# Up products of a convolutional FFN: seven-product pairs in groups of two, and one written order for the end of the stage

## The reference

```python
def conv_ffn(x, w_up, conv_w, conv_b, w_down):      # x 512 x 1024
    h = x @ w_up                                     # 1024 -> 5632
    h = depthwise_causal_conv(h, conv_w) + conv_b    # three taps along the sequence
    gate, val = jnp.split(h, 2, axis=-1)
    return (jax.nn.silu(gate) * val) @ w_down        # 2816 -> 1024
```

## Time and profile before

| | |
|---|---|
| median of 3 runs | 2039.16 us (2037.84 to 2039.9) |
| the profiled execution | 2042.29 us, of which the span from first to last instruction is 2040.6 us |
| PE busy | 2026.4 us, 99% of the span |
| DVE busy | 1619.3 us, 79% |
| ACT busy | 1115.0 us, 55% |
| POOL busy | 433.7 us, 21% |
| granted TensorE clock | full in all 40 slices |

### The profile page before, as it was taken

One profiled execution on the slowest core, in us unless ns is written; L12 is line 12 of the kernel. 1 busy time (PEld: TensorE's weight loads), 2 busy tenths in 40 slices (PEclk: granted clock), 3 DMA queues, 4 the chain that ended last, 5 costly groups with the idle time before them and its releaser, 6 DMA issues.

```text
span 2040.6 us, 33333 instructions
## 1 busy us (share of the span) xinstructions
PE 2026.4 (99%) x12636; PEld 1750.7 (86%) x12636; DVE 1619.3 (79%) x2555; ACT 1115.0 (55%) x1861; POOL 433.7 (21%) x482
## 2 busy tenths in 40 slices
PE   9999999999999999999999999999999999999998
PEld 8889998888988899888877888998888889999887
DVE  6668878889467887899888669777997668877898
ACT  4755545447335555546656646555465755545555
POOL 0520332210000232120035402322110520332220
PEclk9999999999999999999999999999999999999999
DMA  8123344384432334467421123334674122334393
GB/s 291 64 104 125 109 130 150 121 255 172 145 129 75 97 105 129 145 190 243 166 73 42 63 83 104 119 104 155 197 237 163 65 104 83 109 122 147 115 269 122
DMA packets 82570, 276.42 MB, mean 135 GB/s; under 512 B 9408, under 2 KB 13632, under 8 KB 82032
## 3 DMA queue, kind: packets, MB, share of 16 engines
q1 hardware_dynamic: 59184, 214.67, 30.4%
q0 software_dynamic: 11200, 24.12, 5.8%
q10 hardware_dynamic: 12032, 35.54, 4.8%
HBM read 256.43 MB, written 14.73 MB: 133 GB/s over the span
## 4 chain that ended last, share of the span: by engine, by line
PE 91%; DVE 5%; DMA 2%; ACT 1%; issue 0%; DVEq 0%; ACTq 0%; SPq 0%
PE ps L2437 12%; PE ps L2438 12%; PE ps L2439 12%; PE ps L2649 6%; PE ps L3018 5%; PE ps L3019 5%; PE ps L3020 5%; PE ps L2976 5%; PE ps L2978 5%; PE ps L2977 5%; PE ps L2509 2%; PE ps L2465 2%; PE ps L2466 2%; PE ps L2467 2%; DMA raw<-slabs 2%; PE ps L2497 1%
## 5 line engine op out<-in xcount | busy, mean ns | idle before, releaser
L2437 PE MATMUL ps<-h_hi,w_hi 128*128 128x512 f32 (+1 forms) x1104 | 433.0, 392 | 0.0
L2438 PE MATMUL ps<-h_lo,w_hi 128*128 128x512 f32 (+1 forms) x1104 | 429.6, 389 | 0.0
L2439 PE MATMUL ps<-h_hi,w_lo 128*128 128x512 f32 (+1 forms) x1104 | 428.9, 389 | 0.0
L1603 DVE TENSOR_TENSOR w_lo<-raw,w_hi 128x1024 fp32r<-128x1024 f32 x300 | 372.0, 1247 | 39.1 <-ACT w_hi L901 35.5
L901 ACT ACTIVATE w_hi<-raw 128x1024 fp32r<-128x1024 f32 x312 | 326.4, 1053 | 133.1 <-DVE raw L2251 74.0
L2437 PEld LDWEIGHTS ps<-h_hi,w_hi 128*128 128x128 f32 x1104 | 207.6, 188 | 44.0 <-issue 4.0
L2439 PEld LDWEIGHTS ps<-h_hi,w_lo 128*128 128x128 f32 x1104 | 207.3, 188 | 43.2
L2438 PEld LDWEIGHTS ps<-h_lo,w_hi 128*128 128x128 f32 x1104 | 207.7, 188 | 38.9
L1281 ACT ACTIVATE work<-ps,conv_sb 128x512 f32<-128x512 f32 x120 | 93.0, 775 | 162.6 <-PE ps L2439 133.2
L3018 PE MATMUL ps<-w_hi,h_hi 128*128 128x512 f32 x408 | 159.7, 391 | 2.1 <-DVE w_lo L1603 2.1
L3020 PE MATMUL ps<-w_hi,h_lo 128*128 128x512 f32 x408 | 158.8, 389 | 0.0
(11 more groups left out here) (365 smaller groups left out, 5054.6 us busy)
## 6 DMA issues: line engine op xcount, KB each, us to landing
raw<-slabs SPq DMA_DIRECT2D x368, 512.0 KB, 4.1
act<-slabs POOLq DMA_DIRECT2D x64, 256.0 KB, 5.6
bias<-slabs SPq DMA_DIRECT2D x16, 512.0 KB, 6.3
x_dram<-x ACTq DMA_DIRECT2D x16, 512.0 KB, 5.0
x<-x_dram ACTq DMA_DIRECT2D x16, 512.0 KB, 4.9
raw<-act POOLq DMA_DIRECT2D x28, 256.0 KB, 3.3
act<-slabs SPq DMA_DIRECT2D x12, 512.0 KB, 5.4
bias_dram<-bias_rows ACTq DMA_DIRECT2D x2, 2048.0 KB, 12.3
```

The source lines that it names most:

```text
L1603: ve.tensor_tensor(w_lo[:, c % RING, :], raw[:, raw_slot(c), :], w_hi[:, c % RING, :].bitcast(f32), ALU.subtract).then_inc(lo_made, 1)
L2437: pe.matmul(ps[:, bank, cols], hi, h_hi[:, k, cols], start=k == 0, stop=False)
L2438: pe.matmul(ps[:, bank, cols], hi, h_lo[:, k, cols], start=False, stop=False)
L2439: last = pe.matmul(ps[:, bank, cols], lo, h_hi[:, k, cols], start=False, stop=k == KT - 1)
```

## The change

The pairs computed with seven products become 4, 6, 7, 9, 10, 12, 13, 15 and 16: nine per layer in place of seven. Pairs 5, 8, 11, 14 and 17 between them are ordinary. A group is two seven-product pairs f and f+1 and the ordinary pair f+2, and PE interleaves them:

```diff
-FASTS = (FAST_END - FAST) // 2
+FAST_RUNS = 6, 9, 12, 15
+IN_GROUP = 2
+FAST_PAIRS = [FAST] + [q + e for q in FAST_RUNS for e in range(IN_GROUP)]
...
+                p1(FAST)
+                p2(FAST)
+                p6_p5(FAST)
+                p7(FAST)
+                bank_free(FAST + 1)
+                forward(up_slab(L, FAST + 1), 0, up_bank(FAST + 1, 0))
+                p4(FAST)
+                p3(FAST)
+                forward(up_slab(L, FAST + 1, 1), 0, up_bank(FAST + 1, 1))
+                for f in FAST_RUNS:
+                    p1(f)
+                    p2(f)
+                    p6_p5(f)
+                    p7(f)
+                    p1(f + 1)
+                    p2(f + 1)
+                    p4(f)
+                    p3(f)
+                    p6_p5(f + 1)
+                    p7(f + 1)
+                    bank_free(f + 2)
+                    forward(up_slab(L, f + 2), 0, up_bank(f + 2, 0))
+                    p4(f + 1)
+                    p3(f + 1)
+                    forward(up_slab(L, f + 2, 1), 0, up_bank(f + 2, 1))
```

```diff
+                def first_period(f):          # ACT
+
+                    split_hi(up_slab(L, f + 1))
+                    part_hi(f, "x3")
+                    slab_silu(f - 1)
+                    slab_tap(f - 1, 1)
+                    split_hi(up_slab(L, f + 1, 1))
+                    copy(f, 0)
+                    copy(f, 1)
...
+                def period(f):                # DVE, a part
...
+                    part_lo(f + 3, "x1")
+                    part_lo(f + 3, "x3")
+                    slab_gate(f)
+                    part_lo(f + 4, "a11")
+                    slab_tap(f + 1, 1, 1)
+                    c11(f + 3)
+                    x3(f + 4)
+                    slab_tap(f + 1, 1, 0)
+                    c22(f + 3)
...
+                def last_period(f):           # ACT, its end
...
+                    slab_tap(f + 6, 0)
+                    split_hi(DOWN[L] + 2)
+                    operand(L, 3)
+                    slab_silu(f + 6)
+                    slab_tap(f + 6, 1)
+                    split_hi(DOWN[L] + 3)
```

More of the change, by code:

```diff
@@ L709, in _, with load @@
                 ring_slabs(n1 + EARLY, up_slab(L, FAST))
[L710 to L727, removed]
+                def load(q, e):
+                    c = up_slab(L, q, e)
+                    if q - 2 not in FAST_PAIRS:
+                        sp.wait_ge(lo_made, made(c - RAW))
+                    elif e:
+                        sp.wait_ge(part_lo_made["x3"], part_count(L, q - 2, "x3"))
+                        sp.wait_ge(part_lo_made["x4"], part_count(L, q - 2, "x4"))
+                    else:
+                        sp.wait_ge(part_lo_made["x1"], part_count(L, q - 2, "x1"))
+                        sp.wait_ge(up_x2, fast(L, q - 2) + 1)
+                        sp.wait_ge(up_x3, fast(L, q - 2) + 1)
+                    sp.dma_start(raw[:, raw_slot(c), :], slabs[dram(c)]).then_inc(raw_in[raw_slot(c)], 16)
@@ L875, in _ @@
                     at_probs(BASE[L])
-                fourth_sum(L, FAST)
-                for j in range(STEPS - 1):
+                down_sums(L, 0)
+                fourth_sum(L, 4)
+                down_sums(L, 1)
+                fourth_sum(L, 6)
+                fourth_sum(L, 7)
+                down_sums(L, 2)
+                fourth_sum(L, 9)
+                fourth_sum(L, 10)
+                down_sums(L, 3)
+                fourth_sum(L, 12)
+                down_sums(L, 4)
+                fourth_sum(L, 13)
+                down_sums(L, 5)
+                fourth_sum(L, 15)
+                fourth_sum(L, 16)
+                down_sums(L, 6)
+                for j in range(7, STEPS - 1):
                     down_sums(L, j)
-                    if FAST <= 2 * j + 4 < FAST_END and j:
-                        fourth_sum(L, 2 * j + 4)
                 first_sums(L)
@@ new lines, in period @@
+                def period(f):
+                    split_lo(up_slab(L, f + 2))
+                    slab_tap(f - 1, 0, 0)
+                    slab_tap(f, 0, 1)
+                    c11(f + 1)
+                    slab_tap(f - 1, 1, 0)
+                    part_lo(f + 1, "x4")
+                    c22(f + 1)
+                    x1(f + 3)
+                    x1(f + 4)
+                    split_lo(up_slab(L, f + 2, 1))
+                    slab_gate(f - 1)
+                    slab_tap(f, 0, 0)
+                    x2(f + 3)
+                    slab_tap(f, 1, 1)
+                    slab_tap(f + 1, 0, 1)
+                    part_lo(f + 3, "a11")
+                    slab_tap(f, 1, 0)
+                    c12(f + 1)
+                    slab_tap(f + 1, 0, 0)
+                    part_lo(f + 3, "x2")
+                    x3(f + 3)
+                    part_lo(f + 4, "x1")
+                    x2(f + 4)
+                    part_lo(f + 3, "x1")
+                    part_lo(f + 3, "x3")
+                    slab_gate(f)
+                    part_lo(f + 4, "a11")
+                    slab_tap(f + 1, 1, 1)
+                    c11(f + 3)
+                    x3(f + 4)
+                    slab_tap(f + 1, 1, 0)
+                    c22(f + 3)
+                    part_lo(f + 3, "x4")
+                    slab_gate(f + 1)
+                    part_lo(f + 4, "x2")
+                    slab_tap(f + 2, 0, 1)
+                    slab_tap(f + 2, 1, 1)
+                    c12(f + 3)
+                    part_lo(f + 4, "x3")
@@ L2143, in gate, with slab_gate @@
+                def slab_gate(q):
+                    gate(q % 2, q // 2)
                 def gate(c, i):
```

491 lines of the change are left out of this document (318 added, 173 removed).

## The result

| | before | after |
|---|---|---|
| median of the runs | 2039.2 us (2037.84 to 2039.9) | 2053.9 us (2053.21 to 2054.5, 4 runs) |
| ratio, 95% interval | | 1.0073 (1.0055 to 1.009) |
| profiled execution, its span | 2042.3, 2040.6 | 2054.5, 2052.3 |
| mean granted clock | 1.000 | 0.996 |
| matmuls of PE | 12636 | 12924 |

The forecast was 2047.3, with a range from 2042.0 to 2053.5. The direction is right. The time is 6.6 us above the forecast and 0.4 us outside the range, on the side of the first rival, whose figure was 2053.3.

What follows compares the result with a forecast made beforehand. PE, busy 99% of the span, was taken to bound the kernel. Terms of -6.5, +12.1, 0 and +2.5 summed to +8.1 us on the 2039.2 median: 2047.3 us, range 2042 to 2053.5.

Steps and rivals of the forecast that it cites:

- rival 1: PE before p6 of pair 4: the new waits also drop the clock, 6 us more, 2053.3; chance 0.07.
- Term 1: Up stage on PE: two more pairs per layer become cheap, fewer matmuls, 6.5 us saved.
- Term 2: Steady groups of pairs in the up stage: DVE's added work fits with 0.8 us slack, no PE wait, 0.
- Rival 2: Groups in the up stage do not hold, 0.4 us lost in each of 16: +6.4, 2053.7; chance 0.09.
- Term 3: Start of pair 4: ACT's first copy queues behind a waiting SiLU, PE waits 3.0 us per layer, +12.1.
- Rival 3: Start of pair 4: the first copy is not late and p6 starts on time, 2035.2; chance 0.11.
- Term 4: End of up stage: last gate 0.9 us later delays the down product by 0.9, 0.9, 0.7, 0 per layer, +2.5.
- Rival 4: End of the stage helps instead: two present PE waits in the down product vanish, +3.5, 2042.7; chance 0.09.
- The carried difference: Whole kernel: the median taken 3.1 us below the profiled execution, as before the change, so 2050.4 became 2047.3.

Runs made afterwards that it cites:

- e1: The changed kernel with ACT's row at the start of pair 4 put back, first copy ahead of the SiLU: 2040.8 us, ratio 0.9999.
- e4: The changed kernel with the first copy behind SiLU and value tap, ahead of the split: 2049.58 us, ratio 1.0047.
- e7: e1 with the last value tap and last split ahead of operand(L, 3) and the last SiLU at the stage's end: 2034.09 us, ratio 0.9962.
- e11: e7 run once more, on one chip with e9 and e10: 2034.2 us, ratio 0.9968.
- e3: The changed kernel with the first copy right behind the SiLU, ahead of value tap and split: 2044.85 us, ratio 1.0015.
- e6: The changed kernel with 4 more matmuls of 256 columns, result unused, after p2 of pair 4: 2054.34 us, ratio 1.0058.
- e2: The changed kernel with 24 more matmuls of 256 columns, result unused, after p2 of pair 4: 2051.9 us, ratio 1.0057.
- e10: The changed kernel with only the end of the stage changed as in e7, the late first copy left: 2050.84 us, ratio 1.0048.
- e5: The kernel before, with only ACT's row at pair 4 in the changed kernel's order (late first copy): 2056.19 us, ratio 1.0068.
- e8: e7 with POOL's fourth_sum ahead of down_sums again: 2034.5 us, ratio 0.9961.
- e9: e1 run once more, on one chip with e10 and e11: 2040.01 us, ratio 0.9995.

## Why the prediction was wrong in size, by its steps

**Term 1, -6.5: right.** Where no fall comes between (e1 to e4, e7), the stage from p6 to the down product is 1.4 to 1.7 us shorter in each layer (forecast 1.6), and e7 and e11, where nothing else is late, are 8.2 and 6.9 us faster than before by their medians. That holds the 6.5 and a little of the gate that comes earlier.

**Term 2, 0: right.** The period of a group is 31.08 us, the window of a whole group has PE busy throughout, and PE waits nowhere inside the groups. Rival 2 is out. One reading behind this term was wrong, though: full-width low parts do not all stay at 1.22 us beside POOL. In before one takes 1.75 us beside the last of POOL's five instructions for the down product's sums, and beside the same one a half-width part in a group of after takes 1.10 instead of 0.68:

```profile
383.89 1.75 DVE L1603 TENSOR_TENSOR w_lo<-raw,w_hi 128x1024 fp32r<-128x1024 f32 x1
```

```profile
273.96 1.10 DVE L2191 TENSOR_TENSOR a_lo<-raw,a_hi 128x512 fp32r<-128x512 f32 x1
```

That is 0.4 to 0.5 us a time, inside a slack of 0.8; no wait of PE came of it.

**Term 3, +12.1: right in mechanism, place and length.** 2.9 us for 3.0, four times, released by the copy. e3, e4 and e1 take its items away one by one. Rival 3 is out. The rows read 11.6 for the waits themselves, and the distance between the matmuls on both sides gives 12.2.

**The step that failed: pricing these waits at their length.** The prediction kept the clock at its full level because this trace had no wait of that length, put the rival in which the clock drops at 0.07, and sized the sum without it. But a trace with no such wait says nothing for either side. In after the clock falls behind all four waits, 1.4 to 1.5 us each; rival 1 is what happened. That its figure of 1.5 came out is luck: it let the fall last as long as the wait, but after 1.97 us (e4) and 2.44 us (e6) a fall costs the same 1.3 to 1.5. e2 shows the cause (no idle time at p6, no fall there, with all else the same). e3 to e6 and e10 show that falls come with idle times of 2 us and more and not with 1.3, and that from 2 us on the same wait has one or not. "TensorE: Matmul & The Clock Gate" in the Trainium skill, on the clock gate, says that an idle PE falls back to half its clock. The runs agree with the level (0.50 in a window of e5), and the page should have had the larger chance here.

**Term 4, +2.5: the sum right, its layers wrong.** The gate is 0.99 later in every layer (forecast 0.93). The down products of after are longer by 0.47, 0.08, 1.06 and 0.23 us, 1.8 in all, where the forecast had 0.9, 0.9, 0.7 and 0. Over the seven traces with this gate the mean is 2.0, and layer 3, which was to lose nothing, loses most (1.3 on average). So the size came out partly by luck. What failed is the rule that on DVE everything queues behind the gate, with slack that was read in one execution. The split of the earlier trace rows in layer 3 starts 45.98 us after the down product in before, 47.19 in after, and 47.74 in e5, whose gate is where before's is. There DVE had been idle 3 us before that split, waiting for a load of weights:

```profile
1988.58 0.69 DVE L2251 TENSOR_TENSOR raw<-raw 128x512 f32<-128x512 f32 x1 [1.59 <-DMA raw<-slabs]
```

In the other layers the split moves by -0.8 to +1.1 between before and after. A load that lands late takes up the gate's delay or adds its own, so this slack isn't dependable. By the timed pairs the end's order is worth 5 to 6 us for 1.5 us per layer; in proportion 0.99 would cost 3.5 us, an estimate with an interval that holds 2.5. Rival 4 is out: the order helps only with the tap ahead of the operand.

**The carried difference.** The profiled execution of before was 3.1 us above its median, that of after 0.6. Against its own execution the sum gives 2050.4, and 2054.5 was seen: 4.1 short, where the clock alone is 6: the part ahead of the first pair 4 was 1.6 shorter by chance, and the down products lost 0.5 to 0.7 less than term 4. The other 2.5 us of the miss in the median come from this difference, which the prediction carried over as if it belonged to the kernel.

**The account** of the 14.7 us, with sizes from the traces and the timed pairs: groups -6.5, waits +12, clock +6, gate +2 to +3.5. That is +13.5 to +15. The clock's share in the timed runs is an estimate: a mean granted clock below 1 costs that share of the span, and after's runs average 0.9965 where before's average 0.9991 to 0.9998 on the three chips of the experiments, so 5 to 7 us. What stays open is why the same wait of 2.9 us is followed by a fall in one layer and not in another, and where between 2 and 3.5 us the price of the gate lies.

With both ends of the stage in a better order the groups do pay: e7 and e11, at 2034 us, are 0.3 to 0.4% faster than before.

## What to carry to other kernels

In an engine's in-order queue, look first at what an instruction with another engine's product ahead of it holds back: one SiLU that waited for DVE, put ahead of a copy that PE needed, cost 15 us here, more than twice what the change could save. Price a new wait of PE at its length plus a stretch at half clock when it nears 2 us, and see to it that such a wait is filled or cut well below that: 1.3 us was free of it here, and 0.5 us of filling in 2.9 did not prevent it. Look for it in the mean granted clock and in short windows, not in the page's 40 slices. Do not spend slack that was read from a single execution where loads set it.

## What the runs showed of the hardware

The clock behind a wait of PE in otherwise dense matmuls. Falls are counted in the profiled executions (four layers each); the last column is the mean granted clock over all timed runs of each kernel, in the order of the kernels (before: 0.9991 to 0.9998):

| PE idle before p6 | kernels | layers with a fall | mean clock |
|---|---|---|---|
| 0 to 0.04 us | e1, e2, e7, e8, e9, e11 | 0 of 24 | 0.9995, 0.9993, 0.9996, 0.9996, 0.9994, 0.9997 |
| 1.30 us | e3 | 0 of 4 | 0.9994 |
| 1.97 us | e4 | 1 of 4 | 0.9978 |
| 2.44 us | e6 | 4 of 4 | 0.9975 |
| 2.91 us | after, e5, e10 | 8 of 12 | 0.9965, 0.9973, 0.9972 |

By the means, the count of the one profiled execution is too low for e4 and too high for e6 as an average, and no step between 2 and 2.9 us is shown. A fall begins anywhere from 1.0 us before p6's first matmul, still in the wait (e5, layer 0), to 1.5 us after it (after, layer 0). It lasts for 13 to 17 matmuls of 256 columns at 0.213 us instead of 0.120 and costs 1.3 to 1.5 us; once, in e5, it lasted for 27 and cost 2.6 us. It does not grow in step with the wait.

DVE beside POOL: the full-width weight split that takes 1.22 us elsewhere took 1.74 us at 207.73 in after, while POOL was summing, and 1.75 at 383.89 in before. PE did not wait for it in either place. Others, beside the first of POOL's five instructions, stay at 1.22 (212.54 in before). That POOL slows the long ones is read from the overlap; no run tried it.
